# Turning 64x64 blocks for the lower heads of an RWKV scan by TensorE's turning mode

## What is computed

```python
def rwkv7_scan(r, w, k, v, a, b):
    def step(state, inp):
        r_t, w_t, k_t, v_t, a_t, b_t = inp
        sa = jnp.einsum('bhvk,bhk->bhv', state, a_t)
        state = state * w_t[:, :, None, :] + sa[..., None] * b_t[:, :, None, :] \
            + v_t[..., None] * k_t[:, :, None, :]
        return state, jnp.einsum('bhvk,bhk->bhv', state, r_t)
    s0 = jnp.zeros((B, H, N, N), jnp.float32)
    _, ys = lax.scan(step, s0, xs)
```

## Time and profile before

| | us |
|---|---|
| median of 3 runs (2254.86 to 2260.55) | 2256.45 |
| the profiled execution | 2257.62 |
| its span, first to last instruction | 2255.8 |
| the scan, about 754 to 990 us of the span | 236 |

### The profile page before, as it was taken

One profiled execution on the slowest core, in us unless ns is written; L12 is line 12 of the kernel. 1 busy time (PEld: TensorE's weight loads), 2 busy tenths in 40 slices (PEclk: granted clock), 3 DMA queues, 4 the chain that ended last, 5 costly groups with the idle time before them and its releaser, 6 DMA issues.

```text
span 2255.8 us, 35565 instructions
## 1 busy us (share of the span) xinstructions
PE 2135.2 (95%) x15124; PEld 1636.2 (73%) x15124; DVE 1089.7 (48%) x1783; ACT 810.4 (36%) x1359; POOL 329.5 (15%) x407
## 2 busy tenths in 40 slices
PE   7989999999999899987999899989999789999999
PEld 6857888888666799954865674547788567888887
DVE  4255444445666544437234336554353445666532
ACT  3164323224355322233253136662323334222211
POOL 1441000002023200021001016660211011000000
PEclk9999999999999999996999799999999999999999
DMA  4212333232242100001363230012334113322232
GB/s 164 69 41 91 94 95 94 93 99 92 73 154 80 58 4 4 4 5 56 94 172 112 98 103 20 1 47 94 93 94 131 47 37 94 94 94 94 89 96 86
DMA packets 47836, 178.08 MB, mean 79 GB/s; under 512 B 5391, under 2 KB 5903, under 8 KB 46912
## 3 DMA queue, kind: packets, MB, share of 16 engines
q1 hardware_dynamic: 43488, 154.12, 21.5%
q0 software_dynamic: 4192, 21.70, 3.1%
HBM read 166.30 MB, written 10.55 MB: 78 GB/s over the span
## 4 chain that ended last, share of the span: by engine, by line
PE 87%; DVE 6%; ACT 4%; issue 1%; POOL 1%; DMA 0%; SPq 0%; ACTq 0%; DVEq 0%; POOLq 0%
PE ps L295 19%; PE ps L296 19%; PE ps L300 19%; PE ps L2305 8%; PE ps L781 4%; PE ps L1511 3%; PE ps L1259 2%; PE ps L2318 2%; PE ps L1243 1%; PE ps L770 1%; ACT arena L1354 1%; PE ps L1212 1%; DVE arena L1315 1%; PE ps L2671 1%; DVE arena L1299 1%
## 5 line engine op out<-in xcount | busy, mean ns | idle before, releaser
L275 ACT ACTIVATE w_hi<-wring 128x1024 fp32r<-128x1024 f32 (+1 forms) x243 | 254.2, 1047 | 571.2 <-PE ps L300 567.2
L281 DVE TENSOR_TENSOR w_lo<-wring,w_hi 128x1024 fp32r<-128x1024 f32 (+1 forms) x243 | 298.7, 1230 | 296.6 <-ACT w_hi L275 296.0
L295 PE MATMUL ps<-ffn_input_hi,w_hi 128*128 128x512 f32 x352 | 139.5, 396 | 0.0
L296 PE MATMUL ps<-ffn_input_hi,w_lo 128*128 128x512 f32 x352 | 139.1, 395 | 0.0
L2305 PE MATMUL ps<-arena 64*64 64x64 f32 x3712 | 125.1, 218 | 6.4 <-POOL arena L2253 2.8
L2305 PEld LDWEIGHTS ps<-arena 64*64 64x64 f32 x3712 | 120.1, 135 | 13.5 <-issue 11.1
L1401 POOL TENSOR_TENSOR arena<-arena 128x512 f32<-128x512 f32 (+3 forms) x160 | 111.3, 719 | 39.7 <-DVE arena L1307 34.7
L2401 ACT ACTIVATE arena<-ps 128x512 f32<-128x512 f32 x94 | 56.1, 597 | 164.7 <-PE ps L2305 164.7
L295 PE MATMUL ps<-mlp_input_hi,w_hi 128*128 128x512 f32 x256 | 101.6, 397 | 0.0
L295 PE MATMUL ps<-mlp_hi,w_hi 128*128 128x512 f32 x256 | 101.2, 395 | 0.0
L296 PE MATMUL ps<-mlp_input_hi,w_lo 128*128 128x512 f32 x256 | 101.2, 395 | 0.0
(11 more groups left out here) (406 smaller groups left out, 4402.7 us busy)
## 6 DMA issues: line engine op xcount, KB each, us to landing
wring<-weights SPq DMA_DIRECT2D x276, 512.0 KB, 3.5
bias_wide_scratch<-bias_line_scratch POOLq DMA_DIRECT2D x1, 4096.0 KB, 26.5
arena<-bias_wide_scratch POOLq DMA_DIRECT2D x1, 4096.0 KB, 16.8
wring<-weights SPq DMA_DIRECT2D x8, 384.0 KB, 3.1
arena<-x_t SPq DMA_DIRECT2D x4, 512.0 KB, 7.1
xn_scratch<-arena POOLq DMA_DIRECT2D x1, 2048.0 KB, 7.5
x_scratch<-arena POOLq DMA_DIRECT2D x1, 2048.0 KB, 8.3
arena<-xn_scratch POOLq DMA_DIRECT2D x1, 2048.0 KB, 9.1
```

Source lines behind the costliest of these rows:

```text
L275: act.activation(self.w_hi[:, m % SPLIT, 0:n], self.wring[:, g % RING, 0:n], ACT.Copy).then_inc(self.w_hi_ready, 1)
L281: dve.tensor_tensor(self.w_lo[:, m % SPLIT, 0:n], self.wring[:, g % RING, 0:n], self.w_hi[:, m % SPLIT, 0:n].bitcast(F32), ALU.subtract).t ...
L295: pe.matmul(out, hi[:, c, :], src.hi[:, at + c, :], start=(at + c == 0), stop=False)
L296: pe.matmul(out, lo[:, c, :], src.hi[:, at + c, :], start=False, stop=False)
```

## The change

The function `turned(t, x)` takes the place of `product(t, (x, None))` for `vn`, `mn`, `kn` and `bn`. It issues the same 16 matmuls in the same order into the same bank with the same identity; those of the lower heads (`e` = 0) carry `is_transpose=True`, those of the upper heads `is_transpose=False`, as before. No wait, no semaphore, no other engine's code changes, and PE's program has the same 4593 rows of grouped instructions in the same order before and after; only line numbers move.

As built, the two kinds of matmul are not addressed to the array alike. A matmul of the upper head (and before the change of either head) is marked for 64 rows and 64 columns. One with `is_transpose` is marked for rows 0 to 63 and all 128 columns, although its operand has 64. A `pe.transpose` and a turned 64x64 block are one weight load and one matmul instruction each, where another float32 matmul is two of each.

```diff
                 for e in range(2):
                     for i, (lhs, rhs) in enumerate(terms):
-                        right = ident[e * HD:(e + 1) * HD, :] if rhs is None else cut(rhs, p, e)
-                        mm = pe.matmul(cut(out, p, e), cut(lhs, p, e), right, start=(i == 0),
+                        mm = pe.matmul(cut(out, p, e), cut(lhs, p, e), cut(rhs, p, e), start=(i == 0),
                                        stop=(i == len(terms) - 1))
+            mm.then_inc(k.aux_full, 1)
+
+        def turned(t, x):
+
+            k.open_aux(pe, t)
+            out = k.aux(t).rearrange("p (a b) -> p a b", b=CH)
+            for p in range(8):
+                for e in range(2):
+                    mm = pe.matmul(cut(out, p, e), cut(x, p, e), ident[e * HD:(e + 1) * HD, :], is_transpose=(e == 0))
             mm.then_inc(k.aux_full, 1)
...
-                product(t["vn"], (vc, None))
+                turned(t["vn"], vc)
...
-                product(t["mn"], (b["ml1"], None))
+                turned(t["mn"], b["ml1"])
...
-                product(t["kn"], (kc, None))
+                turned(t["kn"], kc)
...
-                product(t["bn"], (bc, None))
+                turned(t["bn"], bc)
```

## The result

The changed kernel takes 2362.1 us (median of 4 runs, 2355.0 to 2365.5) against 2258.5; the ratio is 1.0454, with an interval of 1.0423 to 1.0485. Two executions far slower than their like, one of the kernel before (2675 us) and one of the second experiment (4233 us), stand in none of the figures. The profiled execution took 2365.5 us, its span 2363.7.

A forecast was written before the change was run, and what follows sets the result against it. PE's instruction stream was taken to bound the scan. 2257.6 us for the profiled execution, plus 75.5 for layout changes and 30 for the clock, gave 2363.1; the median being 1.2 lower, 2362 us, range 2313 to 2392.

The forecast's parts named there:

- What bounds the scan: In the scan, PE's instruction stream: all its growth reaches the end, except at most about 5 us vanishing in existing waits.
- Step 1: Turned products' lower heads: one record per float32 block instead of two, 240 removed; hidden, so gain between 0 and 3.5 us.
- Step 2: Layout changes within turned products: a pair of heads takes 431 ns instead of 116.6, +75.5 us over 240 pairs.
- weak joint: In the layout step: no earlier row changes row halves together with layout, yet the full price (+75.5 us) was taken.
- two rivals without a drain: Turned pairs: no layout change felt (2249 to 2256 us; 0.14 including mode not taken up), or serial (2271 us; 0.06).
- Step 3: Granted clock in the scan: thin turned products cause falls to 1.2 GHz, 20 of 1.5 us taken, +30 us (0 to 45).

The follow-up runs named there:

- the second experiment: The kernel before with only the loops of the four turned operands swapped, lower heads first, then upper, no turning mode: 2283.5 us, ratio 1.0091.

## Why the prediction was right

**What bounds the scan.** Borne out. All of PE's growth came to the end: the last copy of y ended at 989.49 us before and at 1094.93 after, the scan began 0.9 us later, so it grew by 104.6 us, and the whole execution by 108 between two profiled runs.

**Step 1, two records become one.** Borne out: 720 records. The saved record was hidden, as was said; in a row of its own it is worth 56 instead of 117 ns.

**Step 2, the layout.** The pair is 428 ns, 431 were worked out: the turning record 172 for 176 (its load open for 25 ns instead of 28), the upper head 107 + 149 for 107 + 148. (3.42 - 0.93) x 30 = 74.7 us for 75.5. The weak joint, that no row of before changed layout between rows of the array that don't overlap, held, and the run with 128 plain columns shows that it is the layout that counts. The two rivals without a drain would have left 0.93 or 1.4 us a product.

**Step 3, the clock.** 104.6 - 74.7 = 29.9 us are left for it, 30 were taken. The mechanism was right; that 20 stretches of 3.4 us came out just as 68.3 / 3.4 is luck, since they were a choice between 0 and 30. They were not 20 falls but 14, and four of them lasted longer, with 6.8 or 10.2 us each, which is the reason that the prediction had given for its choice. 29.9 us in 68.3 us at 1.2 GHz is 0.44 lost in each; from the earlier trace rows it was 1.5 of 3.4, the same. A turned product that stands wholly at 1.2 GHz takes 5.01 for 3.37 us, a factor of 1.5 where a twin's is 1.86: part of the wait between layouts doesn't depend on the clock.

**The sum.** 2363.1 for a profiled execution of 2365.5. The four runs of the changed kernel lie 10 us apart, those of before 8. The slowest of the four had a mean granted clock of 0.957, the fastest 0.961: some 20 us less at 0.50, which at 0.44 is an estimated 9 of the 10 us. So the clock's term itself moves by that much from run to run, and its agreement within 0.1 us is luck.

**What was off.** The price of one half of the array at a time (0.93 us a product expected, 0.61 measured) stood in an experiment and not in the sum; the term was mis-sized because a product was costed as if nothing stood beside its ends. The pair with 128 plain columns was put at 0.56 to 0.60 us and is 0.62: its second record lasts 272 ns and not 218, so the upper head starts 202 ns behind it and not 148.

## What to carry to other kernels

Matmuls in quarters of TensorE's array are cheap because they run side by side; one instruction of another layout (rows or columns claimed) among them ends that twice, once on the way in and once out, here at 90 ns each and 25 to 49 ns for a weight load that nothing hides (102 ns for the plain one of 128 columns). Before changing a small matmul's mode, look at how it claims the array, and if it must differ, put all of the kind in one row: the same 240 turning matmuls cost 103 us alternating and 17 us apart. A stretch of alternating layouts costs again through the clock (0.44 us for each us at 1.2 GHz), and here two of them close together more than twice one.

## What the runs showed of the hardware

A float32 turning matmul of 64 columns costs 56 ns from start to start, half of a plain one in the same quarter (117 ns), and two of them in different halves of the rows start 3 or 4 ns apart, here into different banks. A dense row of them, 128 in 7.33 us, held the full clock. A stretch in which PE is busy without a gap by its records can lose the clock all the same: in the changed kernel PE was busy 3.40 of the 3.40 us up to 779.8, and 10.20 of the 10.20 us at 0.50 behind it.
